# Mixer of a hybrid decoder layer: the next step's first taps before the last softmax difference, whose transposes go into the middle of a projection

## The chip, the cores and the metric

The kernel runs on one core of one Trainium2 chip. The metric is the time of one execution of the program on the device, in microseconds (us). A core has five engines with a queue of instructions each: TensorE (PE, with its weight loads as PEld), VectorE (DVE), ScalarE (ACT), GpSimd (POOL) and SyncE (SP), which here issues nearly all transfers. They wait for each other by semaphores. An engine does its queue in order.

## The reference, cut to what matters

One decoder layer on 512 tokens of width 1024: a combined input projection, differential attention with 8 heads beside a Mamba-2 mixer with 8 groups, a gated merge, and a mixture of 32 experts. The change touches only the part up to the merge. For one attention head and one group of the mixer it computes, cut to the lines that matter:

```python
proj = jnp.einsum('bsd,dc->bsc', h, w_in[l])
xbc = silu(causal_conv4(xbc, conv_w) + conv_b)          # four taps per channel
p = jax.nn.softmax(logits, axis=-1)                     # two maps per head
diff = p[:, :, 0] - lam * p[:, :, 1]
o = jnp.einsum('bhqk,bhkv->bhqv', diff, v)              # then an RMS norm
y = _ssd_scan(xs, dt, a_log, bm, cm) + d_skip * xs      # in four chunks of 128 tokens
y = _rms_norm(y * silu(z), norm_g)
```

## The kernel before, in words

The mixer is a loop of eight steps (`steps_of_mixer`, L388). A step handles one attention head and one group of the Mamba-2 part, for all 512 tokens. Seven steps are one loop body with `more` true, in which the engines also prepare the step i + 1; the eighth has `more` false and prepares nothing.

A step's columns of the input weights come in nine pieces of 128 x 1024 numbers (512 KB). SP loads piece p into one of three buffers once VectorE has done with the piece three before it (L438). ScalarE rounds a piece to its high part (`split`, L516 for pieces 3 to 5 and L524 for the others), VectorE subtracts to get the low part (`split`, L779), and TensorE multiplies three times: high by high, high by low, low by high.

`project(j, n)` (L1040 to L1049) does this for tile n of step j: 24 matmuls of 128 x 512 (L1047) into PSUM bank n % 2. Tiles 0 to 3 are the inputs of the convolution, 4 and 5 are q and k; `project_vz` (L1071) makes v and z. Before a projection `free_proj` (L1030) waits until the bank has been read: tile 2 needs the bank of tile 0, so it waits for `conv_ready` of tile 0. The tiles 0, 1 and 2 of step i + 1 are projected at the end of step i, tile 3 opens the step i + 1.

The convolution of tile n is one instruction of ScalarE (`tap`, L538: bank times the last tap plus bias) and three of VectorE (`taps`, L785: the bank shifted by one, two and three tokens), of which the last signals `conv_ready`. The silu follows on ScalarE (L589).

Attention goes by four blocks u of 128 queries: scores on TensorE (L1105), `logits` on VectorE (L872, L874, the maximum L878 and L879), the exponentials on ScalarE (`softmax_exp`, L633), `make_diff` on VectorE (L892 to L895), which writes the tile `diff`, `turn_diff` on TensorE (L1139: u + 1 transposes of 128 x 128 into the bank m0) and `take_diff` on ScalarE (L641). At the end of the step eight matmul records (L1196) multiply v with the transposed differences into the bank m1; ScalarE squares the result (L717), TensorE sums the squares (L1202), ScalarE takes the root (L721, L722), VectorE scales (L983).

The Mamba-2 part goes by four chunks u: `y_and_state` on TensorE (L1122, L1126, L1131), `sum_y` (L915, L916, L921) and `gate_y` (L928) on VectorE, `norm_y` on ScalarE (L647 to L650, tile `yn`), `turn_y` on TensorE (L1146) and `take_y` on ScalarE (L657). `turn_diff` and `turn_y` share the bank m0, so each also waits until what was there before is taken. `cb` (L1114) multiplies two convolved tiles; for chunk 0 it waits for all four silus.

The order on each engine is written out by hand in the function `body` of that engine. At the end of a step with `more`, before the change, it is:

- TensorE: project(i+1, 1), y_and_state(3), turn_diff(3), project(i+1, 2), turn_y(2), L1196, turn_y(3), L1202, and in the next step project(3), project(4), turn_xb(0), cb(0).
- VectorE: logits(3), gate_y(2), split(i+1, 3), make_diff(3), taps(i+1, 0), sum_y(3), gate_y(3), taps(i+1, 1), splits 4, 5 and 6, taps(i+1, 2), split 7, L983, split 8.
- ScalarE: softmax_exp(3), split(i+1, 4), norm_y(2), tap(i+1, 1), take_diff(3), splits 5 and 6, tap(i+1, 2), take_y(2), norm_y(3), L717, split 7, L721 and L722, take_y(3), split 8.
- SP: the load of piece p of step i + 1 waits for VectorE's split of piece p - 3, then goes the next.

Of the kernel before, what the change touches and what calls it, by code (L numbers as in the profile page):

```python
# [19 lines left out]
KT = D // P  # L20
# [133 lines left out]
def decoder_layer(nc, x, small, consts, onehot_rows, gffn, rel_bias, par, w_mix, w_dt, w_tail, w_rt, w1, w2, b12,  # L154
                  tok_ids, pads, out):
    with ExitStack() as ctx:
# [114 lines left out]
        phi_ready, plo_ready = sig("phi_ready", PIECES), sig("plo_ready", PIECES)  # L271
        bias_in = sig("bias_in", 1, 16)
        proj_done = sig("proj_done", 10)
# [109 lines left out]
        with nc.Block() as block:  # L383
            def piece_of(n):

                return n if n < 3 else n + 3
# [99 lines left out]
            def _(act):  # L486
# [23 lines left out]
                def split(j, p):  # L510

                    act.wait_ge(piece_in[p % MRAW].sem, piece_in[p % MRAW].at(j, p // MRAW + 1))
                    apart(act, eps_ready)
                    if 3 <= p < 6:
                        act.wait_ge(proj_done.sem, proj_done.at(j, 0))
                        act.activation(vz_hi[:, (p - 3) * D:(p - 2) * D], mraw[:, p % MRAW], ACT.Copy).then_inc(  # L516
                            phi_ready.sem, 1)
                        return
                    n = p if p < 3 else p - 3
                    if n >= 3:  # L520
                        act.wait_ge(proj_done.sem, proj_done.at(j, n - 2))
                    elif not isinstance(j, int):
                        act.wait_ge(proj_done.sem, proj_done.at(j - 1, n + 4))
                    act.activation(wm_hi[n % MSPLIT][:].rearrange("p a b -> p (a b)"), mraw[:, p % MRAW],  # L524
                                   ACT.Copy).then_inc(phi_ready.sem, 1)

                def tap(j, n):

                    act.wait_ge(proj_done.sem, proj_done.at(j, n + 1))
                    if n == 3:  # L530
                        act.wait_ge(ydiag_ready.sem, ydiag_ready.at(j, 0))
                    elif not isinstance(j, int):
                        act.wait_ge(m0_ready.sem, m0_ready.at(j - 1, 4))
                        if n == 2:
                            act.wait_ge(m1_ready.sem, m1_ready.at(j - 1, 7))
                    apart(act, eps_ready)
                    p0 = j * NPAR
                    act.activation(conv[:, n], proj_b[n % 2][:], ACT.Identity,  # L538
                                   scale=par_sb[:, bass.ds(p0 + (4 * n + 3), 1)],
                                   bias=par_sb[:, bass.ds(p0 + (16 + n), 1)]).then_inc(taps_ready.sem, 1)  # L540
# [43 lines left out]
                def body(i, more):  # L584
# [52 lines left out]
                    def take_diff(u, k):  # L637
                        act.wait_ge(m0_ready.sem, m0_ready.at(i, k))
                        act.wait_ge(m1_ready.sem, m1_ready.at(i, 0))
                        src = m0_b[:, 0:(u + 1) * P].rearrange("p (a b) -> p a b", a=u + 1)  # L640
                        act.activation(dT[:, 0:u + 1, u * P:(u + 1) * P], src, ACT.Copy).then_inc(m0_read.sem, 1)  # L641

                    def norm_y(u, k):

                        act.wait_ge(y_ready.sem, y_ready.at(i, u + 1))
                        act.wait_ge(m0_ready.sem, m0_ready.at(i, k))
                        ch.link(act.activation(yn[:], ybuf, ACT.Square, accum_out=st[:, 16:17]))  # L647
                        ch.link(act.activation(st[:, 16:17], st[:, 16:17], ACT.Ln, bias=eps[:, 1:2], scale=1.0 / GW))
                        ch.link(act.activation(st[:, 16:17], st[:, 16:17], ACT.Exp, scale=-0.5))
                        act.activation(yn[:], ybuf, ACT.Copy, scale=st[:, 16:17]).then_inc(yn_ready.sem, 1)  # L650
# [54 lines left out]
                    norm_y(2, 9)  # L705
                    if more:
                        tap(i + 1, 1)
                    take_diff(3, 10)
                    if more:
                        split(i + 1, 5)  # L710
                        split(i + 1, 6)
                        tap(i + 1, 2)
                    take_y(2, 11)
                    norm_y(3, 11)

                    act.wait_ge(m1_ready.sem, m1_ready.at(i, 8))
                    act.activation(sq[:, 0], m1_b[:], ACT.Square).then_inc(osq_ready.sem, 1)  # L717
# [20 lines left out]
            def _(dve):  # L738
# [31 lines left out]
                def split(j, p):  # L770

                    dve.wait_ge(phi_ready.sem, phi_ready.at(j, p + 1))
                    if 3 <= p < 6:
                        c = slice((p - 3) * D, (p - 2) * D)
                        hi, lo = vz_hi[:, c], vz_lo[:, c]
                    else:
                        n = (p if p < 3 else p - 3) % MSPLIT
                        hi, lo = (w[n][:].rearrange("p a b -> p (a b)") for w in (wm_hi, wm_lo))
                    dve.tensor_tensor(lo, mraw[:, p % MRAW], hi.bitcast(F32), ALU.subtract).then_inc(plo_ready.sem, 1)  # L779

                def taps(j, n):
                    dve.wait_ge(taps_ready.sem, taps_ready.at(j, n + 1))
                    for s in (1, 2, 3):
                        w = par_sb[:, bass.ds(j * NPAR + (4 * n + 3 - s), 1)]
                        ins = dve.scalar_tensor_tensor(out=conv[:, n, s:T], in0=proj_b[n % 2][:, 0:T - s],  # L785
                                                       scalar=w, in1=conv[:, n, s:T], op0=ALU.mult, op1=ALU.add)
                        if s < 3:
                            ch.link(ins)
                    ins.then_inc(conv_ready.sem, 1)
# [56 lines left out]
                def body(i, more):  # L846
# [118 lines left out]
                    logits(3)  # L965
                    gate_y(2)
                    if more:
                        split(i + 1, 3)
                    make_diff(3, 8)
                    if more:  # L970
                        taps(i + 1, 0)
                    sum_y(3)
                    gate_y(3)
                    if more:
# [25 lines left out]
            def _(pe):  # L1000
# [4 lines left out]
                for b in range(2 * NT):  # L1005
# [4 lines left out]
                    for k in range(4):  # L1010
                        c = t * D + (4 * half + k) * P
                        ins = pe.transpose(hT_bank(b)[:, k * P:(k + 1) * P], xin[:, c:c + P], ident)
# [18 lines left out]
                def free_proj(j, use):  # L1031

                    if use < 2:
                        pe.wait_ge(proj_read.sem, proj_read.at(j, 0))
                    elif use < 6:
                        pe.wait_ge(conv_ready.sem, conv_ready.at(j, use - 1))
                    else:
                        pe.wait_ge(proj_read.sem, proj_read.at(j, use - 5))

                def project(j, n):  # L1040

                    free_proj(j, n)
                    pe.wait_ge(plo_ready.sem, plo_ready.at(j, piece_of(n) + 1))
                    hi, lo = wm_hi[n % MSPLIT], wm_lo[n % MSPLIT]
                    for k in range(KT):
                        for w, h in ((hi, h_hi), (hi, h_lo), (lo, h_hi)):
                            ins = pe.matmul(proj_b[n % 2][:], w[:, k], h[:, k], start=(k == 0 and w is hi and h is h_hi),  # L1047
                                            stop=(k == KT - 1 and w is lo))
                    ins.then_inc(proj_done.sem, 1)  # L1049

                pe.wait_ge(hlo_ready, NT)
                project(0, 0)
# [11 lines left out]
                def body(i, more):  # L1064
# [52 lines left out]
                    def y_and_state(u):  # L1117
                        pe.wait_ge(y_read.sem, y_read.at(i, u))
                        pe.wait_ge(mix_ready.sem, mix_ready.at(i, u + 1))
                        pe.wait_ge(xs_ready.sem, xs_ready.at(i, u + 1))  # L1120
                        for h in range(HPG):
                            ins = pe.matmul(y_b[:, h * HD:(h + 1) * HD], mix[:, h], xdt[:, h * HD:(h + 1) * HD],  # L1122
                                            start=True, stop=True)
                        if u:
                            pe.wait_ge(m1_read.sem, m1_read.at(i, 2 * u))
                            ins = pe.matmul(y_b[:, GW:2 * GW], conv[:, 3, u * P:(u + 1) * P], state, start=True,  # L1126
                                            stop=True)
                        ins.then_inc(ydiag_ready.sem, 1)
                        if u < NT - 1:
                            pe.wait_ge(m1_read.sem, m1_read.at(i, 2 * u + 1))  # L1130
                            pe.matmul(m1_b[:, P:P + GW], xb[:, u, 2 * P:3 * P], xw, start=True, stop=True).then_inc(  # L1131
                                m1_ready.sem, 1)
# [51 lines left out]
                    if more:  # L1184
                        project(i + 1, 1)
                    y_and_state(3)
                    turn_diff(3, 9)
                    if more:
                        project(i + 1, 2)
                    turn_y(2, 10)  # L1190

                    pe.wait_ge(m1_read.sem, m1_read.at(i, 7))
# [843 lines left out]
```

## Time and profile before

| | us |
|---|---|
| median of 3 runs | 2192.01 |
| lowest and highest run | 2190.6, 2192.3 |
| span of the profiled execution | 2190.4 |
| TensorE busy in it | 2057.5 |
| VectorE busy in it | 1583.4 |
| ScalarE busy in it | 1357.9 |
| GpSimd busy in it | 582.6 |

The profiled execution has its span, from its first to its last recorded instruction, and no other time of its own is given. The median of the runs is 1.6 us above the span. The mixer's steps take about 75 to 79 us each and lie in the first 660 us; the experts, from about 1050 us on, take half of the time. In the traces a row of a timeline has its start, its duration, engine, line and tiles, and in brackets how long the engine was idle before it and what ended this.

### The profile page before, as it was taken

The page shows a single profiled execution, that of the slowest core. Times are in us where ns is not written, and L with a number is a line of the kernel's source. Part 1 is how long each engine was busy: PE and PEld are TensorE (multiplying, and loading weights), DVE is VectorE, ACT ScalarE, POOL GpSimd, SP SyncE. Part 2 cuts the span into 40 slices and gives each one's busy share as a digit, 9 for nine tenths or more (in the row PEclk, how much of TensorE's full clock was granted, in tenths as well). Part 3 has the DMA queues.
Part 4 walks back from the last instruction along what each step waited for, and adds up shares of the span by engine and source line. Part 5 has one row for each costly group of instructions (what it writes and reads, how often), then busy time and mean ns, then how long its engine had stood idle before and what let it go on. Part 6 is the DMA issues. An engine that isn't in the chain of part 4 may idle for free.

```text
span 2190.4 us, 30780 instructions
## 1 busy us (share of the span) xinstructions
PE 2057.5 (94%) x9582; PEld 1667.8 (76%) x9582; DVE 1583.4 (72%) x1648; ACT 1357.9 (62%) x1608; POOL 582.6 (27%) x444
## 2 busy tenths in 40 slices
PE   7999999999989999855999999999999999999996
PEld 6877787787767888644788888888888888888885
DVE  5557656755755333334999999999999999999995
ACT  4556656665654222313777777777777777777774
POOL 0211211211120000012225343434434343525251
PEclk8999999999999999966999999999999999999998
DMA  5122112112102222544899999999999999999994
GB/s 180 33 68 89 38 60 79 63 45 69 60 10 97 96 96 96 174 161 171 296 386 370 384 370 386 362 396 362 386 369 380 376 379 377 377 380 377 380 371 151
DMA packets 111577, 509.29 MB, mean 233 GB/s; under 512 B 17936, under 2 KB 21048, under 8 KB 78776
## 3 DMA queue, kind: packets, MB, share of 16 engines
q1 hardware_dynamic: 102712, 479.04, 57.8%
q0 software_dynamic: 8832, 29.84, 6.2%
q8 instruction: 17, 0.28, 0.1%
q14 instruction: 16, 0.13, 0.0%
HBM read 489.01 MB, written 20.91 MB: 233 GB/s over the span
## 4 chain that ended last, share of the span: by engine, by line
PE 52%; DVE 1%; issue 0%; ACT 0%; DMA 0%; POOL 0%; POOLq 0%; ACTq 0%; DVEq 0%
PE bank L1684 32%; PE bank L1697 16%; PE bank L1662 1%; PE bank L1673 1%; PE bank L1708 1%; PE bank L1719 1%; DVE w_lo L1814 0%; DMA keep<-h_rows,g_idx 0%; ACT w_hi L1755 0%; DVE keep L1829 0%; DVE x_lo L1744 0%; DVE keep L1826 0%; DVE keep L1833 0%; POOL out_rows L1903 0%; DVE a_lo L1744 0%
## 5 line engine op out<-in xcount | busy, mean ns | idle before, releaser
L1814 DVE TENSOR_TENSOR w_lo<-big,w_hi 128x2048 fp32r<-128x2048 f32 x384 | 876.2, 2289 | 88.5 <-ACT w_hi L1755 81.5
L1755 ACT ACTIVATE w_hi<-big 128x2048 fp32r<-128x2048 f32 x384 | 736.8, 1920 | 231.6 <-PE bank L1684 176.1
L1684 PE MATMUL bank<-w_hi,x_hi 128*128 128x512 f32 x1024 | 280.3, 396 | 2.6 <-DVE w_lo L1814 2.6
L1684 PE MATMUL bank<-w_lo,x_hi 128*128 128x512 f32 x1024 | 276.0, 391 | 0.0
L1684 PE MATMUL bank<-w_hi,x_lo 128*128 128x512 f32 x1024 | 275.5, 391 | 0.0
L1684 PEld LDWEIGHTS bank<-w_hi,x_hi 128*128 128x128 f32 x1024 | 191.0, 189 | 53.7 <-DVE w_lo L1814 14.7
L1684 PEld LDWEIGHTS bank<-w_lo,x_hi 128*128 128x128 f32 x1024 | 193.3, 189 | 41.1
L1684 PEld LDWEIGHTS bank<-w_hi,x_lo 128*128 128x128 f32 x1024 | 193.2, 189 | 41.0
L1047 PE MATMUL bank<-h_hi,wm_hi 128*128 128x512 f32 x384 | 163.9, 427 | 17.4 <-DVE big L785 12.6
L1892 POOL CAST pick<-pick_rows 128x112 fp32r x65 | 18.2, 280 | 600.1 <-PE bank L1697 575.2
L1697 PE MATMUL bank<-w_hi,a_hi 128*128 128x512 f32 x512 | 162.3, 398 | 0.0
L1697 PE MATMUL bank<-w_lo,a_hi 128*128 128x512 f32 x512 | 158.9, 392 | 0.0
L1697 PE MATMUL bank<-w_hi,a_lo 128*128 128x512 f32 x512 | 158.8, 391 | 0.0
L1897 POOL COPY w_cur<-slots 112x1 f32 x32 | 156.1, 4879 | 4.9 <-DMA out_rows<-keep,s_idx 4.4
L1047 PE MATMUL bank<-h_hi,wm_lo 128*128 128x512 f32 x384 | 154.2, 402 | 0.0
L1047 PE MATMUL bank<-h_lo,wm_hi 128*128 128x512 f32 x384 | 153.6, 400 | 0.0
L474 POOL TENSOR_TENSOR keep<-big,dtv 128x256 f32<-128x256 f32 x32 | 20.8, 648 | 485.1 <-ACT big L621 242.3
L1431 DVE TENSOR_TENSOR g_lo<-keep,g_hi 128x1024 fp32r<-128x1024 f32 x39 | 47.8, 1226 | 125.5 <-ACT g_hi L1356 123.0
L1697 PEld LDWEIGHTS bank<-w_hi,a_hi 128*128 128x128 f32 x512 | 94.1, 189 | 25.9 <-issue 8.0
L1903 POOL DMA_INDIRECT out_rows<-keep,s_idx x32 | 111.6, 3489 | 5.6 <-issue 5.5
L1697 PEld LDWEIGHTS bank<-w_lo,a_hi 128*128 128x128 f32 x512 | 96.6, 189 | 20.6
L1697 PEld LDWEIGHTS bank<-w_hi,a_lo 128*128 128x128 f32 x512 | 96.7, 189 | 20.6
(261 smaller groups left out, 3553.4 us busy)
## 6 DMA issues: line engine op xcount, KB each, us to landing
big<-in_w SPq DMA_DIRECT2D x384, 1024.0 KB, 8.8
big<-in_w_mix SPq DMA_DIRECT2D x72, 512.0 KB, 3.3
keep<-in_w_tail SPq DMA_DIRECT2D x47, 512.0 KB, 3.2
keep<-in_x SPq DMA_DIRECT2D x4, 512.0 KB, 4.9
big<-in_x SPq DMA_DIRECT2D x4, 512.0 KB, 4.9
out_rows<-keep SPq DMA_DIRECT2D x4, 512.0 KB, 3.8
h_rows<-keep SPq DMA_DIRECT2D x4, 512.0 KB, 2.8
bias_rows<-dist_rows SPq DMA_DIRECT2D x1, 1024.0 KB
```

The costliest lines, as they stand in the source:

```text
L1047: ins = pe.matmul(proj_b[n % 2][:], w[:, k], h[:, k], start=(k == 0 and w is hi and h is h_hi), stop=(k == KT - 1 and w is lo))
L1431: dve.tensor_tensor(lo, graw[:, m % GRAW], hi.bitcast(F32), ALU.subtract).then_inc(glo_ready.sem, 1)
L1662: ins = pe.transpose(bank[6 + half][:, k * CAP:(k + 1) * CAP], xg[:, c:c + P], ident[0:CAP, 0:CAP])
L1673: ins = pe.transpose(bank[6 + half][:, k * CAP:(k + 1) * CAP], act_rows[:, c:c + P], ident[0:CAP, 0:CAP])
L1684: ins = pe.matmul(bank[c][:], x_part, w_part[:, s, c * 512:(c + 1) * 512], start=False, stop=n == W1_PAIRS - 1 and w_part is w_hi and x_pa ...
L1697: ins = pe.matmul(bank[4 + c][:], a_part, w_part[:, s, o:o + 512], start=False, stop=k == KT - 1 and w_part is w_hi and a_part is lo)
L1708: pe.matmul(bank[c][:], pick1[r], bias_hl[r, (c % 2) * 512:(c % 2 + 1) * 512], start=True, stop=False)
L1719: pe.matmul(bank[4 + c][:], pick2[r], bias_hl[r, D:D + 512], start=True, stop=False)
L1755: act.activation(w_hi[:, place(b, at_n, SPLIT)], raw[:, place(b, at_n, RAW)], ACT.Copy).then_inc(hi_ready.sem, 1)
L1814: dve.tensor_tensor(w_lo[:, s], raw[:, place(b, at_n, RAW)], w_hi[:, s].bitcast(F32), ALU.subtract).then_inc(lo_ready.sem, 1)
L1897: pool.tensor_copy(w_cur[:], slots[:].bitcast(F32)[:, bass.ds(b, 1), 1:2].rearrange("s a c -> s (a c)"))
L1903: pool.indirect_dma_start(out, bass.IndirectOffsetOnAxis(ap=s_idx[:, 0:1], axis=0), y_rows, None, compute_op=ALU.add).then_inc(scatter_don ...
```

## The change

TensorE: the third projection of the next step is done in two halves of 12 matmuls each, and the transposes of the last difference, which stood before it, are put between the halves. VectorE: the taps of the next step's tile 0 are done before the last difference and the split of piece 3 after it; before, the split came first, then the difference, then the taps. ScalarE: the split of piece 5 is done before the last difference is taken, and the tap of tile 2 after take_y(2) and norm_y(3). No instruction is added or removed.

```diff
@@ ScalarE, body @@
                     norm_y(2, 9)
                     if more:
                         tap(i + 1, 1)
+                    if more:
+                        split(i + 1, 5)
                     take_diff(3, 10)
                     if more:
-                        split(i + 1, 5)
                         split(i + 1, 6)
-                        tap(i + 1, 2)
                     take_y(2, 11)
                     norm_y(3, 11)
+                    if more:
+                        tap(i + 1, 2)
@@ VectorE, body @@
                     logits(3)
                     gate_y(2)
                     if more:
+                        taps(i + 1, 0)
+                    make_diff(3, 8)
+                    if more:
                         split(i + 1, 3)
-                    make_diff(3, 8)
-                    if more:
-                        taps(i + 1, 0)
                     sum_y(3)
@@ TensorE @@
-                def project(j, n):
+                def project(j, n, k0=0, k1=KT):
 
-                    free_proj(j, n)
-                    pe.wait_ge(plo_ready.sem, plo_ready.at(j, piece_of(n) + 1))
+                    if k0 == 0:
+                        free_proj(j, n)
+                        pe.wait_ge(plo_ready.sem, plo_ready.at(j, piece_of(n) + 1))
                     hi, lo = wm_hi[n % MSPLIT], wm_lo[n % MSPLIT]
-                    for k in range(KT):
+                    for k in range(k0, k1):
                         for w, h in ((hi, h_hi), (hi, h_lo), (lo, h_hi)):
                             ins = pe.matmul(proj_b[n % 2][:], w[:, k], h[:, k], start=(k == 0 and w is hi and h is h_hi),
                                             stop=(k == KT - 1 and w is lo))
-                    ins.then_inc(proj_done.sem, 1)
+                    if k1 == KT:
+                        ins.then_inc(proj_done.sem, 1)
@@ TensorE, body @@
                     y_and_state(3)
+                    if more:
+                        project(i + 1, 2, 0, KT // 2)
                     turn_diff(3, 9)
                     if more:
-                        project(i + 1, 2)
+                        project(i + 1, 2, KT // 2, KT)
                     turn_y(2, 10)
```

## Rows read from the trace of the kernel before

**Rows 1.** The page's head.

```profile
span 2190.4 us, 30780 instructions
```

**Rows 2.** Busy time by stretch, the mixer's 60 to 660 us.

```profile
60.00:660.00 600.00, 567.48 (x2774) 454.03 (x2772) 366.73 (x708) 363.42 (x795) 109.00 (x127) 0.98 0.17 55
```

Its columns: stretch and length; busy us of PE, PEld, DVE, ACT and POOL with instructions; granted clock, DMA share, GB/s.

**Rows 3.** Who waited for whom, 60 to 650 us: total, times, longest.

```profile
PE bank L1047 <- DVE big L785: 12.6, 7, 1.8
...
PE bank L1139 <- DVE aux L895: 6.8, 8, 1.6
...
PE bank L1146 <- ACT yn L650: 6.0, 7, 0.9
```

**Rows 4.** Timeline of TensorE, end of the second step.

```profile
192.71 0.65 PE L1126 MATMUL bank<-keep,big 128*128 128x256 f32 x2
194.10 0.65 PE L1139 MATMUL bank<-cst,aux 128*128 128x128 f32 x4 [0.74 <-DVE aux L895]
196.55 0.49 PE L1047 MATMUL bank<-h_hi,wm_hi 128*128 128x512 f32 x1 [1.80 <-DVE big L785]
...
202.12 0.38 PE L1146 MATMUL bank<-cst,yn 128*128 128x128 f32 x2
...
205.52 0.43 PE L1146 MATMUL bank<-cst,yn 128*128 128x128 f32 x2 [0.86 <-ACT yn L650]
205.93 1.12 PE L1202 MATMUL bank<-keep,cst 128*128 128x512 f32 x2
...
219.04 0.39 PE L1114 MATMUL bank<-big 128*128 128x128 f32 x2
```

**Rows 5.** Busy time over the third projections of seven steps, columns of rows 2.

```profile
117.67:126.01 8.34, 8.34 (x24) 6.57 (x25) 7.04 (x10) 1.12 (x2) 0.00 (x0) 0.65 0.22 71
196.55:202.12 5.57, 5.57 (x24) 4.56 (x25) 5.07 (x9) 1.13 (x2) 0.00 (x0) 1.00 0.00 0
272.73:279.95 7.22, 7.22 (x24) 5.70 (x25) 6.72 (x10) 1.13 (x2) 0.00 (x0) 0.76 0.12 33
...
sum 46.64, PE 46.64 PEld 37.38 DVE 42.33 ACT 7.87 POOL 0.00; mean PE 6.66 PEld 5.34 DVE 6.05 ACT 1.12 POOL 0.00
```

**Rows 6.** Timeline of VectorE, end of the second step.

```profile
190.86 1.22 DVE L779 TENSOR_TENSOR vz_lo<-big,vz_hi 128x1024 fp32r<-128x1024 f32 x1
192.30 0.17 DVE L892 RECIPROCAL st<-st 128x2 f32<-128x2 f32 x1 [0.22 <-ACT aux L633]
...
193.89 0.74 DVE L785 SCALAR_TENSOR_TENSOR big<-bank,par_sb,big 128x511 f32<-128x511 f32 x1
194.78 1.64 DVE L785 SCALAR_TENSOR_TENSOR big<-bank,par_sb,big 128x510 f32<-128x510 f32 x2 [0.15 <-DVE big L785]
196.34 0.41 DVE L915 TENSOR_TENSOR big<-bank,keep 128x256 f32<-128x256 f32 x1
...
202.87 1.22 DVE L779 TENSOR_TENSOR wm_lo<-big,wm_hi 128x1024 fp32r<-128x1024 f32 x1
```

**Rows 7.** Timeline of SP: the issue of the load of piece 6.

```profile
192.24 0.33 SPq L438 DMA_DIRECT2D big<-in_w_mix  x1
```

**Rows 8.** Transfers issued from 190 to 195 us: KB, us from issue to landing.

```profile
big<-in_w_mix SPq DMA_DIRECT2D x1, 512.0 KB, 3.2
```

**Rows 9.** Timeline of ScalarE, from the end of the second step.

```profile
196.62 1.06 ACT L524 ACTIVATE wm_hi<-big 128x1024 fp32r<-128x1024 f32 x1
202.60 0.78 ACT L538 ACTIVATE big<-bank,par_sb 128x512 f32<-128x512 f32 x1 [4.92 <-PE bank L1047]
203.28 0.62 ACT L657 ACTIVATE keep<-bank,par_sb 128x128 f32 x2
...
205.30 0.58 ACT L717 ACTIVATE keep<-bank 128x512 f32<-128x512 f32 x1
205.78 1.05 ACT L524 ACTIVATE wm_hi<-big 128x1024 fp32r<-128x1024 f32 x1
...
216.42 0.63 ACT L589 ACTIVATE big<-big 128x512 f32<-128x512 f32 x1 [2.73 <-DVE big L785]
```

**Rows 10.** The page's transfers of the expert stage: KB, us from issue to landing.

```profile
big<-in_w SPq DMA_DIRECT2D x384, 1024.0 KB, 8.8
```

More of the change, by code:

```diff
@@ L967, in body @@
                     if more:
-                        split(i + 1, 3)
+                        taps(i + 1, 0)
                     make_diff(3, 8)
                     if more:
-                        taps(i + 1, 0)
+                        split(i + 1, 3)
                     sum_y(3)
```

## The prediction

> **What bounds the kernel now.** I read the page first: the span is 2190.4 us [rows 1]. Then the windows: of the 600 us of the mixer, TensorE is busy 567.48 us, VectorE 366.73 and ScalarE 363.42 [rows 2]. So TensorE sets the time there, and only what shortens TensorE's own row of work counts. Then the list of waits, for what TensorE waits for: the first matmul of a projection waited 12.6 us on VectorE's L785, seven times, 1.8 us at most; the transposes of the softmax difference (L1139) 6.8 us on L895, eight times; the transposes of yn (L1146) 6.0 us on ScalarE's L650, seven times [rows 3]. Seven is the number of steps that prepare a next one. The reader should see that these are waits on the order in which VectorE and ScalarE do their work, for neither is full.
>
> TensorE's timeline of the second step [rows 4] shows the place: the last y matmul ends at 192.71 + 0.65 = 193.36; 0.74 us idle; four transposes of the difference at 194.10; 1.80 us idle; the third projection at 196.55; transposes of yn at 202.12, then the matmuls of the attention output; 0.86 us idle; transposes of yn again at 205.52; L1202 at 205.93. The projection waits for its PSUM bank: bank 0 is free only once VectorE's taps(i+1, 0) have read it.
>
> There is a second price. The windows over the third projection, one for each of the seven steps, show it 5.57 us long at a granted clock of 1.00, but 8.34 us at 0.65 in the first step and 7.22 us at 0.76 in the third [rows 5]: part of it ran at the lower level, 1.2 GHz. Four of seven steps show this, always right behind the 1.80 us idle, never behind the 0.86 us idle. The sum row gives 46.64 us for the seven, against 7 x 5.57 = 38.99: 7.65 us is what the clock costs here.
>
> **The change, part by part**, with the second step's times as the example.
>
> VectorE. split(3) starts at 190.86, the difference at 192.30, taps at 193.89 (three instructions, until 196.42), sum_y at 196.34 [rows 6]. Now taps come first, at 190.86; their operands are long there, since ScalarE's tap(i+1, 0) and the first projection are done before. Taps take 196.34 - 193.89 = 2.45 us of the queue, their end releases TensorE 196.55 - 193.89 = 2.66 us after their start: TensorE may begin the projection at 193.52, 0.16 us after its y matmuls. The difference starts at 193.31 and is ready for TensorE 194.10 - 192.30 = 1.80 us later, 195.11. split(3) follows at 193.31 + 1.59 = 194.90 and ends at 196.12. sum_y then starts about 196.04, 0.30 us earlier than now: the queue no longer waits before the difference. All behind it is the same work: split(6) ends at 204.09 - 0.30 = 203.79.
>
> TensorE. Half of the projection (12 of 24 matmuls, 2.8 us) ends about 196.3, and the difference has been ready for 1.2 us: no wait. The four transposes go into another PSUM bank and cost between 0.23 us (128 columns each against 512, a quarter of 5.57 / 24, four times) and the 0.65 us of their row; I take 0.65, the row of this very group. The projection then ends at 193.52 + 5.57 + 0.65 = 199.74 instead of 202.12: 2.38 us.
>
> ScalarE and the weight queue. Two things were moved past others. split(i+1, 5) goes ahead of take_diff(3); its piece is loaded long before, and take_diff has nobody waiting until the attention output. Nothing. But VectorE's split(3) ends 4.04 us later, and SP's load of piece 6 waits for it: it was issued at 192.24, 0.16 us after that split [rows 7], so after the change at 196.28, and it lands 3.2 us after issue [rows 8], at 199.48. ScalarE's split(i+1, 6), before at 196.62 and 1.06 us long [rows 9], must wait for it and hands the engine on 0.10 us ahead of its own end (as L717, 0.58 us from 205.30, does at 205.78), at 200.44. Behind it in ScalarE's queue is take_y(2), which could start at 199.74 + 0.38 of transposes + 0.15 of release (VectorE's to TensorE is 0.13) = 200.27: it is 0.17 us late.
>
> The tail. In the kernel before, ScalarE does tap(2) at 202.60, take_y(2) at 203.28, norm_y(3), and the squares of L717 at 205.30 [rows 9]. From take_y to L717 are 2.02 us; with the tap (0.68 us) moved behind norm_y, 2.70. So yn comes earlier and TensorE's 0.86 us wait on L650 shrinks by the 0.68 of the tap; but L1202, next in TensorE's queue, waits for L717, 0.63 us after its start, and L717 stands behind the tap as before. That part gives nothing: the wait moves from L1146 to L1202. L717 starts at 200.44 + 2.70 = 203.14, L1202 at 203.77 instead of 205.93. The gain of a step is 2.15 us. Its ends: 1.75 (a load 0.4 us longer) and 2.75 (cheap transposes and a load that is never waited for: 193.52 + 5.57 + 0.23 = 199.32, and 0.53 + 2.70 + 0.63 behind it, 203.18).
>
> What is next late? Projection(i+1, 3) wants piece 6 at about 204.3; split(6) ends at 203.79. That fits by 0.5 us. Piece 7: its load is issued after split(4), 0.3 us earlier than now, lands near 204.9, and ScalarE is ready for it at 203.15 + 0.48 = 203.63, where before it took it at 205.78 [rows 9]. ScalarE therefore waits 1.2 us and everything behind moves earlier by 0.9 instead of 2.15. The silu(3) of the following step, which ended at 216.42 + 0.63 = 217.05 [rows 9], ends at 216.15; TensorE's L1114, before at 219.04 [rows 4], wants it at 216.89. Hidden, with 0.7 us left. taps(i+1, 2) start after split(6), as they nearly do now, and fit before projection(i+1, 4).
>
> The clock. With 0.16 us idle in place of 0.74 and 1.80, TensorE works nearly without a break; the idle of the tail stays where the clock never fell. I take all 7.65 us back. Both ends: 0 and 7.65, and below nothing if falls appear at new places; the three full-speed steps make the upper end likelier. The Trainium skill (TensorE: Matmul & The Clock Gate, section on HAM oscillation) blames longer idle gaps than this one for a fall. By that rule the 1.80 us would not be the cause, the falls would stay, and the sum would be 15.05 alone.
>
> Sum: 7 x 2.15 = 15.05, and 7.65: 22.7 us. The last step prepares nothing and is not changed, nor is anything after the mixer. Against the profiled span of 2190.4 that is 2167.7; the trace shows nothing of what lies around the span, and the median of the runs is 2192.0, 1.6 us more. Against that: 2169.3.
>
> **The rivals.**
>
> The clock stays (0.13). The falls have another cause, or come in the tail instead. For it: three steps with the same idle did not fall, so the idle alone does not decide. Against it: every fall of the middle steps lies in this projection. Time: 2192.0 - 15 = 2177.
>
> ScalarE's queue gives the wait on (0.08). The late pieces 6 and 7 hold take_y(2) or silu(3) longer than I reckon; the margins are 0.2 too little and 0.7 us. With 1 us more of it in each step the idle comes back into the tail: 2192.0 - 7 x 1.15 and part of the clock, 2178 to 2184. Against it: VectorE and ScalarE wait in many places of the next step.
>
> Nothing changes (0.04). The difference isn't ready in the middle, so the transposes wait there what they waited before: 2192. The 1.2 us margin speaks against it.
>
> Slower (0.03). The load of piece 6, issued 4 us later, is what decides, through ScalarE's split(6) ahead of take_y(2). Beyond 3.2 us each us of its flight goes straight to L1202. At 3.2 + 2.15 = 5.35 us from issue to landing the gain is gone; at the 8.8 us of the copies of the expert stage [rows 10] each step loses 3.45 us, 24 us in all: 2216. Against it: those copies are twice as large and in a stage that fills the DMA engines.
>
> **How the numbers follow.** The forecast, both terms within their ends, has 0.72: 2169.3, itself 2165 (7 x 2.75) to 2172 (7 x 1.75). The range adds the case of the clock and reaches 2164 to 2178; what is left out is most of the second rival, no change and slower. A measurement of this kernel can tell about 0.2%, 4.4 us. Faster is 0.72 + 0.13 + 0.08 and 0.01 for what I haven't named: 0.94; same 0.03, slower 0.03.
>
> **What would show it.** In the profile of the changed kernel: the wait of L1047 on L785 near 0.2 us a step instead of 1.80; L1139 without a wait, between two halves of the projection; the wait of L1146 on L650 down to about 0.4, and a new one of L1202 on L717 of about 0.7; from one step's y matmuls (L1126) to L1202 about 11.1 us instead of 13.2; a granted clock of 1.00 in all seven third projections. It would be wrong if L1202 or L1047 waited over 1 us, if a clock of 0.65 to 0.76 stood there still, or if ScalarE's L524 waited for a DMA of over 4 us.

## The result and the profile after

The median of the changed kernel is 2169.53 us (four runs, 2167.78 to 2171.31) against 2191.31 us (four runs, 2189.1 to 2192.3) before it: a ratio of 0.9896, with a 95% interval of 0.9885 to 0.9908, 21.8 us less by the medians. (The ratios and intervals here are the comparison's own figures, from all runs; the two medians by themselves give 0.9901, which lies inside the interval.) In the second comparison further down, the same two kernels gave 2168.97 and 2190.77, again 21.8 us, with a ratio of 0.9899 (0.9883 to 0.9914).

The page of the changed kernel, its head and the busy time:

```profile
span 2169.1 us, 30780 instructions
...
PE 2052.2 (95%) x9582; PEld 1664.2 (77%) x9582; DVE 1581.6 (73%) x1648; ACT 1357.3 (63%) x1608; POOL 584.5 (27%) x444
```

The instructions are the same in number, and VectorE and ScalarE are as busy as before; TensorE is busy 5.3 us less, and the span is 21.3 us shorter. The rest of the gain, 16.0 us, was idle time of TensorE. (Lines behind the edits have moved: L1047 is L1050 now, L1139 is L1143, L1146 is L1150, L1196 is L1202, L1202 is L1208, L785 is L787, L717 is L719. The lines of the experiments lie one to three beside these.)

Who waited for whom from 60 to 650 us (us in total, times, longest us), beside [rows 3]:

```profile
ACT wm_hi L524 <- DMA big<-in_w_mix: 21.6, 14, 2.0
...
PE bank L1143 <- DVE aux L897: 5.0, 2, 3.5
PE bank L1208 <- ACT keep L719: 4.9, 8, 0.7
PE bank L1150 <- ACT yn L650: 4.1, 7, 0.6
...
PE bank L1050 <- DVE big L787: 1.3, 7, 0.2
```

TensorE's 12.6 us before the third projection are 1.3; the wait for yn is 4.1 instead of 6.0, and a new one of 4.9 us stands before the sum of squares. The transposes of the difference (L1143) still wait twice, 1.57 and 3.47 us, but both times in the eighth step, which prepares nothing and has no projection to put around them; before the change it had the same two waits. In the seven other steps they wait for nothing. ScalarE now waits for weights, twice a step.

TensorE's timeline at the end of the second step, beside [rows 4]:

```profile
188.90 0.65 PE L1130 MATMUL bank<-keep,big 128*128 128x256 f32 x2
189.74 0.49 PE L1050 MATMUL bank<-h_hi,wm_hi 128*128 128x512 f32 x1 [0.18 <-DVE big L787]
...
192.59 0.60 PE L1143 MATMUL bank<-cst,aux 128*128 128x128 f32 x4
192.95 0.48 PE L1050 MATMUL bank<-h_hi,wm_hi 128*128 128x512 f32 x1
...
195.81 0.38 PE L1150 MATMUL bank<-cst,yn 128*128 128x128 f32 x2
...
198.93 0.43 PE L1150 MATMUL bank<-cst,yn 128*128 128x128 f32 x2 [0.58 <-ACT yn L650]
200.02 1.12 PE L1208 MATMUL bank<-keep,cst 128*128 128x512 f32 x2 [0.66 <-ACT keep L719]
```

The transposes stand between two halves of the projection and wait for nothing. From the y matmuls to the sum of squares are 200.02 - 188.90 = 11.12 us, where they were 205.93 - 192.71 = 13.22.

VectorE, ScalarE and SP in the same stretch, beside [rows 6, 9, 7]:

```profile
187.08 0.74 DVE L787 SCALAR_TENSOR_TENSOR big<-bank,par_sb,big 128x511 f32<-128x511 f32 x1
187.97 1.64 DVE L787 SCALAR_TENSOR_TENSOR big<-bank,par_sb,big 128x510 f32<-128x510 f32 x2 [0.15 <-DVE big L787]
189.53 0.16 DVE L894 RECIPROCAL st<-st 128x2 f32<-128x2 f32 x1
...
191.10 1.22 DVE L781 TENSOR_TENSOR vz_lo<-big,vz_hi 128x1024 fp32r<-128x1024 f32 x1
...
198.77 1.22 DVE L781 TENSOR_TENSOR wm_lo<-big,wm_hi 128x1024 fp32r<-128x1024 f32 x1
```

```profile
195.73 1.06 ACT L524 ACTIVATE wm_hi<-big 128x1024 fp32r<-128x1024 f32 x1 [1.90 <-DMA big<-in_w_mix]
196.69 0.61 ACT L657 ACTIVATE keep<-bank,par_sb 128x128 f32 x2
...
198.70 0.78 ACT L538 ACTIVATE big<-bank,par_sb 128x512 f32<-128x512 f32 x1
199.38 0.59 ACT L719 ACTIVATE keep<-bank 128x512 f32<-128x512 f32 x1
201.15 1.06 ACT L524 ACTIVATE wm_hi<-big 128x1024 fp32r<-128x1024 f32 x1 [1.19 <-DMA big<-in_w_mix]
```

```profile
192.49 0.33 SPq L438 DMA_DIRECT2D big<-in_w_mix  x1
```

From its taps to its split of piece 6 VectorE waits for no other engine; before, it waited 0.22 us for the exponentials ahead of the difference. The load of piece 6 goes out at 192.49, and ScalarE starts its split 3.24 us later.

The granted clock over the third projections (busy us by engine, then the clock), beside [rows 5]; the seven rows are alike, and the sum is 42.49 us for seven stretches that now hold the transposes too:

```profile
115.72:121.79 6.07, 6.04 (x28) 4.96 (x29) 5.55 (x10) 3.35 (x8) 0.00 (x0) 1.00 0.26 86
189.74:195.81 6.07, 6.07 (x29) 4.95 (x29) 5.53 (x10) 3.31 (x7) 0.00 (x0) 1.00 0.27 86
```

None of them falls to the lower level, where four of seven did.

### The profile page after: what moved, and what is told of

Its sections match the earlier page's. It is cut to its first block, busy times and chain, and to the rows that moved or that the text cites. A ratio compares the mean times of both kernels' runs of the same rounds, so it can differ in the third digit from the quotient of the medians.

```text
span 2169.1 us, 30780 instructions
## 1 busy us (share of the span) xinstructions
PE 2052.2 (95%) x9582; PEld 1664.2 (77%) x9582; DVE 1581.6 (73%) x1648; ACT 1357.3 (63%) x1608; POOL 584.5 (27%) x444
## 4 chain that ended last, share of the span: by engine, by line
PE 52%; DVE 1%; issue 0%; ACT 0%; DMA 0%; POOL 0%; POOLq 0%; ACTq 0%; DVEq 0%
PE bank L1690 33%; PE bank L1703 16%; PE bank L1668 1%; PE bank L1679 1%; PE bank L1714 1%; PE bank L1725 1%; DVE w_lo L1820 0%; DMA keep<-h_rows,g_idx 0%; ACT w_hi L1761 0%; DVE keep L1835 0%; DVE x_lo L1750 0%; DVE keep L1832 0%; DVE keep L1839 0%; POOL out_rows L1909 0%; DVE a_lo L1750 0%
## 5 line engine op out<-in xcount | busy, mean ns | idle before, releaser
L1050 PE MATMUL bank<-h_hi,wm_hi 128*128 128x512 f32 x384 | 162.1, 422 | 4.4 <-DVE h_lo L770 3.1
L1050 PE MATMUL bank<-h_hi,wm_lo 128*128 128x512 f32 x384 | 152.2, 396 | 0.0
L1050 PE MATMUL bank<-h_lo,wm_hi 128*128 128x512 f32 x384 | 151.6, 395 | 0.0
```

## The experiments

The theory (A in the texts on record): the new order takes 2.15 us from each of seven steps, the rest comes from the clock, which fell where TensorE had been idle; and what is left of the waits depends on ScalarE's chain behind the third projection and on the load of piece 6. The rivals are named with each run. To compare kernels within a step, I use the step length: the time from one group of attention-output matmuls (L1196 before, L1202 after) to the next, from the second to the seventh step, divided by five. It leaves out the start of the program, which differs by some us from one profile to the next (more below).

| kernel | median us | ratio to before, 95% | step length us | projections or tails with a fallen clock |
|---|---|---|---|---|
| before | 2191.31 | 1 | 77.15 (76.17 where the clock holds) | 4 of 7 |
| after | 2169.53 | 0.9896, 0.9885 to 0.9908 | 74.02 | 0 |
| TensorE's part undone | 2178.42 | 0.9939, 0.9924 to 0.9954 | 75.18 | 0 |
| VectorE's part undone | 2198.41 | 1.0024, 1.0014 to 1.0034 | 78.29 | 6 of 7 |
| ScalarE's part undone | 2167.36 | 0.9890, 0.9873 to 0.9907 | 74.01 | 0 |
| before, idle filled | 2183.54 | 0.9964, 0.9951 to 0.9976 | 76.07 | 0 |
| difference after the projection | 2175.08 | 0.9922, 0.9908 to 0.9935 | 74.72 | 0 |
| split 3 first | 2172.82 | 0.9926, 0.9912 to 0.9940 | 74.79 | 0 |
| split 3 late | 2196.81 | 1.0024, 1.0013 to 1.0035 | 77.38 | 6 of 7 |
| tap after the squares | 2165.35 | 0.9876, 0.9861 to 0.9891 | 73.39 | 0 |
| split 2 early | 2166.62 | 0.9873, 0.9858 to 0.9888 | 73.25 | 0 |
| both | 2159.74 | 0.9849, 0.9835 to 0.9862 | 72.59 | 0 |

The first four experiments shared the runs of the kernel before (median 2193.19), the next three and a second run of the changed kernel did (2190.77), and so did the last three (2193.93). So the ratios are what to compare, and where their intervals overlap, the step lengths. A step length and a count of falls come from one profiled execution of each kernel.

**TensorE's part undone.** To the changed kernel:

```diff
                     y_and_state(3)
-                    if more:
-                        project(i + 1, 2, 0, KT // 2)
                     turn_diff(3, 9)
                     if more:
-                        project(i + 1, 2, KT // 2, KT)
+                        project(i + 1, 2)
```

> TensorE's part is undone: the transposes of the difference stand before the whole third projection again; the orders of VectorE and ScalarE are the new ones. Theory A (the order gives 2.1 us a step, the clock the rest, and the halving is what hides the difference): after the y matmuls (end at 189.55 us in the second step of the changed kernel) TensorE waits until the difference is ready at 189.53 + 1.80 = 191.33, transposes, and the projection ends 1.8 us later than in the changed kernel; 0.35 us of that comes back, because take_y(2) no longer stands behind the load of piece 6. 7 x 1.45 = 10 us over the changed kernel: 2179.5, if the clock holds through an idle of 1.8 us, up to 2187 if it falls as before the change. Theory C (the gain came from VectorE's taps being early, the halving gives nothing): 2169.5, within 2 us.

Measured 0.9939, 2178.42 us. Its timeline of TensorE in the second step and the clock over the third projection:

```profile
186.98 0.65 PE L1130 MATMUL bank<-keep,big 128*128 128x256 f32 x2
189.38 0.65 PE L1143 MATMUL bank<-cst,aux 128*128 128x128 f32 x4 [1.75 <-DVE aux L897]
...
199.22 1.13 PE L1206 MATMUL bank<-keep,cst 128*128 128x512 f32 x2 [0.66 <-ACT keep L719]
```

```profile
189.78:195.35 5.57, 5.57 (x28) 4.55 (x26) 5.07 (x9) 2.28 (x3) 0.00 (x0) 1.00 0.27 94
```

TensorE waits 1.75 us for the difference, once, and a step is 1.16 us longer than with the halves, where I expected 1.45. So the halving is worth 1.16 us of the step's 2.15, and theory C falls. Of the gain of this kernel over the one before, 76.17 - 75.18 = 0.99 us a step is order. The clock held in all seven steps through 1.74 to 1.77 us of idle in one piece.

**VectorE's part undone.**

```diff
                     if more:
-                        taps(i + 1, 0)
-                    make_diff(3, 8)
-                    if more:
                         split(i + 1, 3)
+                    make_diff(3, 8)
+                    if more:
+                        taps(i + 1, 0)
```

> VectorE's part is undone: split(3), difference, taps; TensorE's halves and ScalarE's new order stay. Theory A: the projection can't start until the taps have read the bank, about 192.7 us in the second step, so TensorE is idle for 3.2 us in one piece, the transposes come after it in the middle, and a step is 0.5 us longer than in the kernel before: 2192 + 4 = 2196 with falls of the clock as in the kernel before, and more, to 2205, if the longer idle makes the clock fall in each of the seven projections. Theory C (the halving alone frees TensorE of the wait on the difference, so a part of the gain stays): 2187, 0.74 us a step under the kernel before.

Measured 1.0024 (1.0014 to 1.0034), 2198.41 us: slower than the kernel before. TensorE's wait in the second step, and the third projection of the first, the second and the third step:

```profile
197.38 0.49 PE L1050 MATMUL bank<-h_hi,wm_hi 128*128 128x512 f32 x1 [3.18 <-DVE big L787]
```

```profile
117.86:126.71 8.85, 8.85 (x28) 7.06 (x29) 6.86 (x10) 1.55 (x2) 0.00 (x0) 0.66 0.25 78
```

```profile
197.38:203.44 6.06, 6.06 (x28) 4.95 (x29) 5.56 (x9) 1.55 (x2) 0.00 (x0) 1.00 0.00 0
274.10:281.73 7.63, 7.63 (x28) 6.15 (x29) 6.88 (x10) 1.54 (x2) 0.00 (x0) 0.78 0.16 51
```

The halves alone join two waits to one of 3.18 us, behind which the clock falls in six of seven steps. The step that holds its clock is 76.73 us long, 0.56 over the 76.17 before, as expected (0.5). TensorE's part without VectorE's is a loss of 0.24%, and theory C, which kept a part of the gain, falls.

**ScalarE's part undone.**

```diff
-                    if more:
-                        split(i + 1, 5)
                     take_diff(3, 10)
                     if more:
+                        split(i + 1, 5)
                         split(i + 1, 6)
+                        tap(i + 1, 2)
                     take_y(2, 11)
                     norm_y(3, 11)
-                    if more:
-                        tap(i + 1, 2)
```

> ScalarE's part is undone: the tap of tile 2 ahead of take_y(2) again, the split of piece 5 behind take_diff(3). Theory A (the wait only moved from the transposes of yn to the sum of squares): 2169.5, within 1.5 us; TensorE waits 1.2 us a step for yn and nothing for the squares, in place of 0.58 and 0.66. Theory D (ScalarE's order is worth the 0.28 to 0.68 us by which yn came earlier): 2171.5 to 2174.3.

Measured 0.9890 (0.9873 to 0.9907), a step length of 74.01 against 74.02 us: the part moves no time. The median of 2167.36 is 0.6 us outside the 1.5 us that I had allowed, on the side away from theory D, which asked for more than 2171.5 and falls. TensorE's timeline of the second step:

```profile
199.56 0.43 PE L1148 MATMUL bank<-cst,yn 128*128 128x128 f32 x2 [1.18 <-ACT yn L650]
199.97 1.13 PE L1206 MATMUL bank<-keep,cst 128*128 128x512 f32 x2
```

The 1.18 us stand before the transposes of yn, and nothing before the sum of squares; with the part in, it is 0.58 and 0.66. It is one wait, in one place or in two.

**The kernel before with its idle filled.** To the kernel before:

```diff
                     turn_diff(3, 9)
                     if more:
+                        pe.wait_ge(plo_ready.sem, plo_ready.at(i + 1, 3))
+                        pe.wait_ge(decay_ready.sem, decay_ready.at(i, 4))
+                        for k in range(7):
+                            pe.matmul(seg_b[:], wm_hi[2][:, k], h_hi[:, k], start=True, stop=True)
                         project(i + 1, 2)
```

> The kernel before with seven more matmuls of 128 x 512 put between the transposes of the last difference and the third projection of the next step, where TensorE waited 1.80 us for its bank; their result is not used. They take about 1.6 us and so change no wait. Theory A (the idle there is what lets the clock fall): a granted clock of 1.00 in all seven third projections, 5.57 us each, and 7.65 us less: 2184. Theory B (the falls have another cause): 46.6 us for the seven projections as before, 2191 to 2192.

The two waits that stand ahead of the extra matmuls are for the weights that they read and for the bank that they write. Measured 0.9964 (0.9951 to 0.9976), 2183.54 us, against 2193.19 of the kernel before in the same comparison. TensorE's timeline of the second step, and one of the seven windows over the third projection with the sum of them:

```profile
192.11 0.65 PE L1139 MATMUL bank<-cst,aux 128*128 128x128 f32 x4 [0.75 <-DVE aux L895]
192.51 1.87 PE L1192 MATMUL bank<-h_hi,wm_hi 128*128 128x512 f32 x7
194.48 0.51 PE L1047 MATMUL bank<-h_hi,wm_hi 128*128 128x512 f32 x1
```

```profile
118.39:123.96 5.57, 5.57 (x24) 4.55 (x25) 5.07 (x9) 1.19 (x2) 0.00 (x0) 1.00 0.00 0
...
sum 38.99, PE 38.99 PEld 31.84 DVE 35.49 ACT 8.33 POOL 0.00; mean PE 5.57 PEld 4.55 DVE 5.07 ACT 1.19 POOL 0.00
```

TensorE does seven more matmuls a step and the program is faster. The projections take 38.99 us in all where they took 46.64: 7.65 us, and the ratio gives 0.0036 x 2191 = 7.9 us (5.3 to 10.7). A step of 76.07 us is the 76.17 of the steps before that kept their clock. So the clock's part of the gain is shown by itself: it goes when the 1.80 us of idle are filled with work, and theory B falls. Whether the missing idle or the added work keeps the clock up, this run can't tell apart, and the run with TensorE's part undone shows that such an idle stretch alone does not lower it. The Trainium skill (TensorE: Matmul & The Clock Gate, HAM oscillation) warns of longer idle gaps than these. Here the clock fell with no gap over 1.80 us around it, so keeping below the page's figure was not enough.

**The changed kernel again.**

> The changed kernel once more, as the measure for the three beside it: 2169.5, within 2 us; a ratio of 0.990 to the kernel before.

Measured 2168.97 us, a ratio of 0.9899, a step length of 73.98 us.

**The difference after the whole projection.**

```diff
                     y_and_state(3)
                     if more:
-                        project(i + 1, 2, 0, KT // 2)
+                        project(i + 1, 2)
                     turn_diff(3, 9)
-                    if more:
-                        project(i + 1, 2, KT // 2, KT)
```

> The changed kernel with the third projection whole again and the transposes of the difference behind it, before those of yn. Theory A (they belong in the middle, because the transposes of yn and the attention output wait for ScalarE to take the difference out of the bank): TensorE waits about 0.9 us a step for take_diff(3), and L1208 comes 0.9 us later: 2169.5 + 6.5 = 2176. Rival E (ScalarE waits for the load of piece 6 anyway, so the later difference is hidden): 2169.5 to 2171.

Measured 0.9922 (0.9908 to 0.9935), 2175.08 us, 0.70 us a step more than the changed kernel, where I expected 0.9. Rival E (2169.5 to 2171) falls. The transposes of yn now wait for ScalarE to empty the bank that they share with the difference, in the second step:

```profile
195.96 0.60 PE L1143 MATMUL bank<-cst,aux 128*128 128x128 f32 x4
197.25 0.44 PE L1150 MATMUL bank<-cst,yn 128*128 128x128 f32 x2 [0.69 <-ACT big L641]
```

Beside their place in the middle, where they cost their own time and no wait, the transposes cost 1.16 us a step more ahead of the projection and 0.70 more behind it.

**Split 3 first.**

```diff
                     if more:
+                        split(i + 1, 3)
                         taps(i + 1, 0)
                     make_diff(3, 8)
-                    if more:
-                        split(i + 1, 3)
                     sum_y(3)
```

> The changed kernel with VectorE's split of piece 3 ahead of the taps. The load of piece 6 goes out 2.8 us earlier, the taps end 1.14 us later. Theory A: TensorE is idle for 1.3 us before the third projection, of which 0.35 us comes back because ScalarE's split of piece 6 no longer holds take_y(2): 7 x 0.8 = 5.5 us more, 2175, with the clock at 1.00; if the clock falls at 1.3 us of idle, up to 2183. Rival F (the late load is what bounds the tail, so the earlier load is worth more than the later taps cost): under 2169.5.

Measured 0.9926 (0.9912 to 0.9940), 2172.82 us, 0.77 us a step more than the changed kernel, where 0.8 was expected. Its list of waits of TensorE, 60 to 650 us, and the window over the third projection of the second step:

```profile
PE bank L1049 <- DVE big L787: 9.2, 7, 1.3
```

```profile
188.31:194.38 6.07, 6.07 (x28) 4.95 (x29) 5.50 (x11) 3.12 (x4) 0.00 (x0) 1.00 0.03 11
```

The taps are late by the split, and TensorE waits 1.33 us where it waited 0.18; the load is early, and the wait for yn is 0.23 us in place of 0.58. That gives 0.35 of the 1.15 us back, and 0.80 is left. Rival F falls. The clock held through 1.33 us in all seven steps.

**Split 3 late.**

```diff
                     make_diff(3, 8)
-                    if more:
-                        split(i + 1, 3)
                     sum_y(3)
                     gate_y(3)
                     if more:
+                        split(i + 1, 3)
                         taps(i + 1, 1)
```

> The changed kernel with VectorE's split of piece 3 behind gate_y(3), so that the load of piece 6 goes out 1.8 us later. It tests the slower rival of the prediction: each us by which the piece lands later goes to the sum of squares on TensorE. Theory A: ScalarE's split of piece 6 starts 1.8 us later, L1208 1.8 us later, 7 x 1.8 = 12.6 us: 2182, and more if the idle of 3 us in the tail makes the clock fall in the fourth projection, up to 2195. Rival E (there is slack in the tail): 2169.5 to 2173.

Measured 1.0024 (1.0013 to 1.0035), 2196.81 us, 1.8 us over the upper end of what I had written. The waits from 60 to 650 us:

```profile
ACT wm_hi L524 <- DMA big<-in_w_mix: 25.6, 7, 3.8
PE bank L1149 <- ACT yn L650: 16.5, 7, 2.5
```

and TensorE in the second step, with a window of 8 us over the end of that step:

```profile
199.08 0.38 PE L1149 MATMUL bank<-cst,yn 128*128 128x128 f32 x2
...
204.00 0.68 PE L1149 MATMUL bank<-cst,yn 128*128 128x128 f32 x2 [2.38 <-ACT yn L650]
205.09 2.08 PE L1207 MATMUL bank<-keep,cst 128*128 128x512 f32 x2 [0.41 <-ACT keep L719]
```

```profile
202.00:210.00 8.00, 5.59 (x12) 3.49 (x13) 5.37 (x7) 6.65 (x15) 0.00 (x0) 0.62 0.74 225
```

The wait for yn rose from 0.58 to 2.38 us, by 1.80 us; counted from the y matmuls, the split of piece 3 on VectorE and that of piece 6 on ScalarE are each 1.82 us later. So nearly all of the time by which piece 6 lands later goes to TensorE, and rival E falls: it is the mechanism of the prediction's slower rival, made true. To that comes the clock, which now falls in the tail, in six of seven steps. The one step that kept it is 75.67 us long, 1.65 over the changed kernel's 74.02 and still 0.50 under the 76.17 of the kernel before: by the step lengths, this version would not be slower without the falls.

**The tap after the squares.** To the changed kernel:

```diff
                     norm_y(3, 11)
-                    if more:
-                        tap(i + 1, 2)
                     act.wait_ge(m1_ready.sem, m1_ready.at(i, 8))
                     act.activation(sq[:, 0], m1_b[:], ACT.Square).then_inc(osq_ready.sem, 1)
                     if more:
+                        tap(i + 1, 2)
                         split(i + 1, 7)
```

> The changed kernel with ScalarE's tap of tile 2 behind the squares of the attention output, not ahead of them. Theory A (L1208 waits for the squares, and the squares stand behind the tap): the squares come 0.68 us earlier, TensorE's wait of 0.66 us before L1208 goes, but then the fourth projection meets VectorE's split of piece 6, which ends at 199.99 us in the second step where the projection would start at 199.92: 0.46 us a step, 3.2 us in all: 2166 where the changed kernel has 2169.2. Rival G (the tap is on no path there either, since the taps on VectorE get later by as much): no change, 2169.

Measured 0.9876 (0.9861 to 0.9891), 2165.35 us, 0.63 us a step less than the changed kernel, where 0.46 was expected; rival G falls. Its TensorE in the second step: the sum of squares follows the transposes without a wait, and then the next projection starts 0.77 us later instead of 0.56, because of VectorE's split of piece 6.

```profile
197.23 0.43 PE L1149 MATMUL bank<-cst,yn 128*128 128x128 f32 x2 [0.50 <-ACT yn L650]
197.64 1.13 PE L1207 MATMUL bank<-keep,cst 128*128 128x512 f32 x2
198.41 0.58 PE L1049 MATMUL bank<-h_hi,wm_hi 128*128 128x512 f32 x1
```

I had taken those 0.2 us off in every step; over the seven steps they were between nothing and 0.22 us, which is part of why the gain is larger.

**Split 2 early.** To the changed kernel:

```diff
                     make_diff(2, 6)
+                    if more:
+                        split(i + 1, 2)
                     sum_y(2)
-                    if more:
-                        split(i + 1, 2)
```

> The changed kernel with VectorE's split of piece 2 ahead of sum_y(2), in the 1.50 us in which VectorE waits there for ScalarE. All that VectorE does behind it up to the taps, and the load of piece 6, comes 1.4 us earlier. Theory A (VectorE's row of work from the logits to the split of piece 6 is what bounds the two places that are left): the 0.18 us ahead of the third projection and the 0.36 us by which the load of piece 6 holds take_y(2) go: 0.54 us a step, 2165.4. Rival H (TensorE alone bounds the step now, what it still waits for is ScalarE's chain from take_y(2) to the squares, which starts with TensorE): 0.18 us a step at the most, 2168.

Measured 0.9873 (0.9858 to 0.9888), 2166.62 us, 0.77 us a step less than the changed kernel, where 0.54 was expected; rival H (0.18 at the most) falls. TensorE now goes from the y matmuls into the projection without a wait:

```profile
188.30 0.65 PE L1130 MATMUL bank<-keep,big 128*128 128x256 f32 x2
188.60 0.59 PE L1050 MATMUL bank<-h_hi,wm_hi 128*128 128x512 f32 x1
```

The projection starts 0.30 us after the y matmuls, not 0.84 as in the changed kernel. The idle of 0.18 us in the profile was counted from the modelled end of the matmuls, and going without it gives more than it says: 0.54 us, of which the projection, 6.17 us long in place of 6.07, takes 0.10 back. The wait for yn is 0.23 us in place of 0.58. 0.54 - 0.10 + 0.35 = 0.79.

**Both edits together.**

> Both edits together. Theory A: they add up, and since VectorE's split of piece 6 is now 1.2 us earlier the tap gives its whole 0.66 us: 0.54 + 0.66 = 1.2 us a step, 8.4 us in all, 2160.8; a step of 72.8 us in place of 74.0. If Rivals G and H hold: 2168 to 2169.

Measured 0.9849 (0.9835 to 0.9862), 2159.74 us, 1.43 us a step less than the changed kernel; 0.63 + 0.77 = 1.40, so the two edits add up. Of TensorE's waits at the end of the second step one is left:

```profile
196.55 0.43 PE L1149 MATMUL bank<-cst,yn 128*128 128x128 f32 x2 [0.23 <-ACT yn L650]
```

This version is faster than both kernels: its interval lies below that of the change, 0.9885 to 0.9908.

## Why the prediction was right

It said 2169.3 us, in a range of 2164 to 2178; measured were 2169.5. Step by step:

- **The order, 2.15 us a step.** Shown: 76.17 - 74.02 = 2.15. Its parts in the second step, in the times of the kernel before less 3.81 us (the y matmuls start that much earlier in this profile): projection from 189.71, measured 189.74; end of the projection 195.93, measured 195.81, because the transposes in the middle cost 6.07 - 5.57 = 0.50 us and not 0.65 (that I took a little too much here was made up for on ScalarE, below); ScalarE's split of piece 6 at 195.67, measured 195.73; sum of squares at 199.96, measured 200.02.
- **The clock, 7.65 us.** Shown in two ways, by no fall in the changed kernel and by the filled one. What I wrote of its cause was too narrow: I put the falls down to the 1.80 us of idle. With TensorE's part undone there are 1.75 us in one piece and the clock never fell. In the kernel before it is 0.74 and 1.80 us on either side of four short transposes. The filled kernel took away the larger one and that was enough. Which of the two stretches decides in a given step, and why three of seven steps escaped, no run here was made to tell. The term of 7.65 us rested on the 1.80 us as the cause, which the run with TensorE's part undone does not bear out, so that it came out whole is in part luck.
- **The wait of 0.86 us that only moves.** Shown by ScalarE's part undone: 1.18 us in one place or 0.58 and 0.66 in two, and the same step.
- **The late load of piece 6.** Shown: ScalarE waits 1.90 us for it, and piece 7 holds ScalarE for 1.19 us, where I had 1.2. It costs TensorE little because it comes soon after take_y(2) could start: 0.53 us behind the projection's end at 195.81 would be 196.34, and it started at 196.69, so it was 0.35 us late where I had 0.17. That is why the wait for yn is 0.58 us and not the 0.4 that I named. Of the further 1.82 us of delay in the run with split 3 late, 1.65 came through.
- **The rivals.** The clock did not stay low. "Nothing changes" and "ScalarE's queue gives the wait on" did not occur; the margin of the difference (ready 1.2 us before the middle) was enough. The slower rival's mechanism is real: with piece 6 1.8 us later, the kernel is slower than before, though only with the falls of the clock that come with it. The chances that I named for the cases add up to 1.00 with 0.04 for no change, and in the last sum no change has 0.03 and the unnamed 0.01; the two lists don't agree by that hundredth.

Seven times 2.15 and 7.65 are 22.7 us; the medians give 21.8, the ratio (0.0104 x 2191) 22.8 with an interval of 20.2 to 25.2, and the profiles 21.3. From the first step's end to the last step's, y_and_state(3) to y_and_state(3), the profiles do give 22.67: 647.40 - 112.98 before, 625.83 - 114.08 after. Of the missing 1.4 us of the profiles, 0.3 lie behind the last step and 1.1 in the start of the program, which the change doesn't touch and where the clock was lower in this profile, the kernel before first, the changed one second:

```profile
10.00:110.00 100.00, 93.14 (x460) 77.06 (x459) 59.05 (x113) 52.03 (x104) 14.63 (x17) 0.91 0.28 89
```

```profile
10.00:110.00 100.00, 94.42 (x456) 77.39 (x455) 58.10 (x110) 52.17 (x104) 13.58 (x16) 0.88 0.26 87
```

The end of the first step differs by such amounts between profiles of kernels that are the same up to there (the first group of attention-output matmuls stands at 122.01 and at 123.37 us in two profiles of the changed kernel), so I take this for the clock's chance there and not for a cost of the change. That is an argument and not shown. That the prediction came within 0.3 us of the median is partly luck.

## What to carry to other kernels

Where an engine waits twice in a row on another, ask what the second engine could do in a different order, and put the piece that is ready late into the middle of a long run of work that is ready early; one half of such an edit alone can be a loss, as TensorE's was here without VectorE's, while VectorE's and ScalarE's without TensorE's kept 0.6% of the 1.0%. Then follow what was moved: a transfer whose issue waits for the moved instruction lands later by as much, and it holds all that stands behind its consumer in that engine's queue. A wait on an engine may have two prices, its length and the slower clock behind it: look at the clock in windows over the work behind the wait, and fill such a gap with matmuls whose result is not used to learn the second price by itself.

## What the runs showed that I had not expected

- Seven more matmuls a step made the kernel before faster by 0.36% (0.24 to 0.49).
- A single idle stretch of 1.75 us in every step, or one of 1.33, left the clock at 1.00 in all seven steps, while 0.74 and 1.80 us around 0.65 us of transposes lost it in four of seven, and 3.18 us in one piece in six of seven.
- An idle stretch that the profile gives as 0.18 us was worth more than that when it went: the next matmul followed 0.30 us after the start of the row before it, not 0.84, and the projection took 0.10 us more, so 0.44 us came of it.
- The eighth step still waits 3.47 us for the last difference, in both kernels; no run took that up.
